# Reading w_ada's second third between the last six projections, and its last third behind the second scores

## What is computed

```
mod = silu(c) @ w_ada + b_ada            # w_ada: 1024 x 6144, 24 MB
sh_m, sc_m, gt_m, sh_f, sc_f, gt_f = split(mod, 6)
h    = rms_norm(x, g_pre_mix) * (1 + sc_m) + sh_m
proj = h @ w_in                          # q, k, v of branch a (8 heads) and of branch b (8 heads), forget gates
mix  = concat(fox_attention(a), moba_attention(b))
x    = x + gt_m * rms_norm(mix @ w_out, g_post_mix)
h    = rms_norm(x, g_pre_ffn) * (1 + sc_f) + sh_f
y    = mixture_of_experts(h)             # 32 experts, 4 of them per token, 12 MB of weights each
x    = x + gt_f * rms_norm(y, g_post_ffn)
```

## Time and profile before

| | |
|---|---|
| median of three runs | 2179.22 us (2178.69 to 2185.49) |
| span of the profiled execution | 2178.5 us (its device time is not listed apart; the span is 0.7 us under the median) |
| PE busy | 2000.2 us, 92% |
| DVE busy | 798.3 us, 37% |
| ACT busy | 704.7 us, 32% |
| DMA | 609.45 MB, mean 280 GB/s |
| mean granted TensorE clock | 0.963 |

### The profile page before, as it was taken

One profiled execution on the slowest core, in us unless ns is written; L12 is line 12 of the kernel. 1 busy time (PEld: TensorE's weight loads), 2 busy tenths in 40 slices (PEclk: granted clock), 3 DMA queues, 4 the chain that ended last, 5 costly groups with the idle time before them and its releaser, 6 DMA issues.

```text
span 2178.5 us, 30306 instructions
## 1 busy us (share of the span) xinstructions
PE 2000.2 (92%) x11645; PEld 1302.6 (60%) x11646; DVE 798.3 (37%) x1335; ACT 704.7 (32%) x1092; POOL 261.4 (12%) x246
## 2 busy tenths in 40 slices
PE   4997899999999999999999789997999799997998
PEld 2874433333333333333333388986998689987996
DVE  2544211111111111112111266416775474246763
ACT  1543112122222211111211246514554455315543
POOL 3400100000000010001000002000332020001340
PEclk7998699999999999999999989998999899998999
DMA  9956799998996999899999755434555454353553
GB/s 357 319 211 256 279 417 417 417 418 323 415 418 282 418 417 417 325 418 417 417 417 418 313 177 174 155 116 155 174 180 188 123 182 143 122 193 119 191 177 114
DMA packets 203055, 609.45 MB, mean 280 GB/s; under 512 B 10522, under 2 KB 115118, under 8 KB 166384
## 3 DMA queue, kind: packets, MB, share of 16 engines
q1 hardware_dynamic: 197600, 585.40, 70.3%
q0 software_dynamic: 5040, 21.89, 2.8%
q10 hardware_dynamic: 328, 0.95, 0.1%
HBM read 607.13 MB, written 9.26 MB: 283 GB/s over the span
## 4 chain that ended last, share of the span: by engine, by line
PE 70%; DMA 11%; DVE 5%; issue 5%; SPq 5%; ACT 3%; DVEq 0%; ACTq 0%
PE bank L744 32%; PE bank L1002 15%; PE bank L1031 9%; DMA ring<-in_w_gate_up 7%; PE bank L1095 3%; PE bank L962 2%; SPq L625 2%; SPq L628 2%; DMA ring<-in_w_in 2%; PE bank L975 1%; PE bank L995 1%; ACT probs L1587 1%; DMA ring<-in_w_ada 1%; DVE split L1424 1%; DVE probs L1152 1%
## 5 line engine op out<-in xcount | busy, mean ns | idle before, releaser
L1002 PE MATMUL bank<-ring,qkv 128*64 128x512 f32 x2240 | 496.6, 597 | 13.3 <-DMA ring<-in_w_gate_up 13.3
L744 PE MATMUL bank<-hT_hi,split 128*128 128x256 f32 x2432 | 442.7, 285 | 5.1 <-DVE hT_lo L1432 4.0
L744 PEld LDWEIGHTS bank<-hT_hi,split 128*128 128x128 f32 x2432 | 382.5, 194 | 7.9 <-issue 6.7
L1424 DVE TENSOR_TENSOR split<-ring,split 128x2048 fp32r<-128x2048 f32 x120 | 283.8, 2367 | 265.4 <-ACT split L1745 265.2
L1745 ACT ACTIVATE split<-ring 128x2048 fp32r<-128x2048 f32 x120 | 229.6, 1913 | 416.4 <-PE bank L744 327.8
L1002 PEld LDWEIGHTS bank<-ring,qkv 128*64 128x64 f32 x2240 | 155.3, 137 | 337.6 <-issue 294.8
L744 PE MATMUL bank<-hT_lo,split 128*128 128x256 f32 x1216 | 345.8, 284 | 0.0
L1031 PE MATMUL bank<-ring,qkv 128*64 128x512 f32 x1120 | 255.8, 598 | 25.7 <-ACT qkv L1706 23.5
L744 PEld LDWEIGHTS bank<-hT_lo,split 128*128 128x128 f32 x1216 | 235.2, 193 | 0.0
L1402 DVE SCALAR_TENSOR_TENSOR out_halves<-bank,probs,out_halves 64x512 fp32r<-64x512 f32 x70 | 52.5, 750 | 395.2 <-ACT out_halves L1728 394.7
L1392 DVE TENSOR_SCALAR qkv<-bank 128x512 f32<-128x512 f32 x35 | 24.2, 692 | 422.9 <-PE bank L1002 422.9
(11 more groups left out here) (284 smaller groups left out, 2278.7 us busy)
## 6 DMA issues: line engine op xcount, KB each, us to landing
ring<-in_w_gate_up SPq DMA_DIRECT2D x256, 1024.0 KB, 17.0
ring<-in_w_down SPq DMA_DIRECT2D x150, 1024.0 KB, 15.7
ring<-in_w_in SPq DMA_DIRECT2D x58, 1024.0 KB, 5.6
ring<-in_w_up SPq DMA_DIRECT2D x44, 1024.0 KB, 5.1
ring<-in_w_ada SPq DMA_DIRECT2D x24, 1024.0 KB, 8.3
ring<-in_w_out SPq DMA_DIRECT2D x12, 1024.0 KB, 6.4
ring<-in_w_branch SPq DMA_DIRECT2D x12, 1024.0 KB, 5.0
neighbours<-rpb_copies POOLq DMA_DIRECT2D x32, 128.0 KB, 8.4
```

Source lines behind the costliest of these rows:

```text
L744: last = pe.matmul(out, a[a_half], b[b_half], start=start and i == 0, stop=stop and i == 2)
L1002: last = pe.matmul(hidden[q][CAP * j:CAP * j + CAP, :], xgT[:, k % 4, k // 4, :], unit_at(k)[:, c:c + 512], start=False, stop=(k == KC - 1))
L1424: dve.tensor_tensor(low, unit_at(u % RING_L), high.bitcast(F32), ALU.subtract).then_inc(low_done, 1)
```

## The change

The order of the 40 units becomes: 8 of `ada0`; w_in's first six; then `qb0`, two of `ada1`, `qb1`, two of `ada1`, `kb0`, two, `kb1`, one, `vb0`, one, `vb1`; 8 of `ada2`; 4 of w_out. TensorE uses them in that order. The rows of `ada1` follow the scores of branch b, with all of `ada2` behind them and ahead of the values of b; the rows of `ada2` come between the second and the third unit of the product with w_out. VectorE copies the sums of `ada1` before `out_low("a")`, makes its rows between `keep_scores("b")` and `normalise`, and all four rows of `ada2` before `post_norm`. The sums of `ada1` move from `htok` to a part of `qkv`. The first expert's units wait slot by slot, and are issued in the order of slots 4, 5, 0, 1, 2, 3, then 8 to 11, then 6 and 7.

```diff
+FIRST_PART = 6
+BESIDE = dict(zip(IN1[FIRST_PART:], ((0, 2), (2, 4), (4, 6), (6, 7), (7, KC), (KC, KC))))
+
+def first_order():
+    order = [("ada0", k) for k in range(KC)] + [("in", u) for u in range(FIRST_PART)]
+    for u in range(FIRST_PART, len(IN1)):
+        order += [("in", u)] + [("ada1", k) for k in range(*BESIDE[IN1[u]])]
+    return order + [("ada2", k) for k in range(KC)] + [("out", u) for u in range(OUT_UNITS)]
+
+ORDER_1 = first_order()
+SPLIT_1 = [u for u, (kind, _) in enumerate(ORDER_1) if kind in ("in", "out")]
...
-        modrows = [probs_t[:, 2048:2560], htok_t[:, 0:512], qkv[:, 0:512]]
+        modrows = [probs_t[:, 2048:2560], qkv[:, 512:1024], qkv[:, 0:512]]
...  SP
+            sources = [parts[kind][i] for kind, i in ORDER_1]
...
             def first_wait(u):
-                if u == 0:
+                if u < RING:
+                    sp.wait_ge(unit_done, 1 + max(n for n in range(first.units) if n % RING == u))
+                if u == KC:
                     sp.wait_ge(unit_done, first.units)
                 if u == RING:
                     sp.wait_ge(h_ready, 4)
                     sp.wait_ge(*emptied("mod11"))
-            load_expert(0, first_wait)
+            ring_order = [n % RING for n in range(first.units - RING, first.units)]
+            load_expert(0, first_wait, [*ring_order, *range(KC, MOE_UNITS), *range(RING, KC)])
...  PE
             scores("a", proj1["qa"], lambda h, o: proj1["ka"][o:o + DH, h // 2, :], fox_bias)
-            project_set(IN1[6:])
+            for n in IN1[FIRST_PART:]:
+                project_set([n])
+                if BESIDE[n][0] < BESIDE[n][1]:
+                    ada_units(1, range(*BESIDE[n]))
             values("a", lambda h, c: proj1["va"][:, c, h * DH:h * DH + DH])
...
             scores("b", proj1["qb"], lambda h, o: proj1["kb"][o:o + DH, h // 2, :])
-            ada(1)
+            ada_rows(1)
+            ada_units(2, range(KC))
             values("b", lambda h, c: proj1["vb"][:, c, h * DH:h * DH + DH])
-            ada_units(2, range(KC // 2))
 
             def mixed_in(u):
+                if u == OUT_UNITS // 2:
+                    ada_rows(2)
                 read(*[f"{'ab'[u // 2]}out{2 * (u % 2) + i}" for i in range(2)])
 
             split_rows_product("mix", lambda f: (mix_hi[:, f, :], mix_lo[:, f, :]), KC, mixed_in)
-            ada_units(2, range(KC // 2, KC))
-            ada_rows(2)
...  DVE
             first_low(8, 9, 10, 11)
+            ada_sums(1)
...
             keep_scores("b", lambda tt, h: tables[:, tt, h, :])
+            ada_rows(1, 2 * [gate(gate_m, gpost_m)] + 2 * [shift(shift_f)])
             normalise()
-            ada(1, 2 * [gate(gate_m, gpost_m)] + 2 * [shift(shift_f)])
+            ada_sums(2)
             first_low(len(IN1), len(IN1) + 1)
             out_low("b")
             first_low(len(IN1) + 2, len(IN1) + 3)
+            ada_rows(2, 2 * [gain(gain_f, gpre_f)] + 2 * [gate(gate_f, gpost_f)])
+            await_own("mod5")
             post_norm([f"mix{j}" for j in range(4)], gate_m, x_mid)
-            ada(2, 2 * [gain(gain_f, gpre_f)])
+            await_own("mod7")
             await_own("mod9")
             await_x_mid()
             row_scale()
             modulated(gain_f, shift_f)
-            ada_rows(2, 2, 2 * [gate(gate_f, gpost_f)])
```

More of the change, by code:

```diff
@@ L203, in project, with project_beside, after_scores @@
             p.unit(n)
-    ada(0)
+    def project_beside():
+        p.bank("ada1")
+        for n in IN1[FIRST_PART:]:
+            project([n])
+            for k in range(*BESIDE[n]):
+                p.unit("ada1")
+    def after_scores():
+        ada_rows(1)
+        ada_units(2, KC)
+    ada_units(0, KC)
+    ada_rows(0)
     for l in range(LAYERS):
@@ L212, in plan_first @@
     p.tile("forget")
[L213 to L216, removed]
+    project(IN1[2:FIRST_PART])
+    p.attention("a", project_beside)
+    p.attention("b", after_scores)
     for j in range(4):
@@ L598, in _ @@
             w_out_v = w_out[0].rearrange("(k p) n -> p k n", p=P)
[L599 to L604, removed]
+            parts = {f"ada{r}": [w_ada[0, P * k:P * k + P, r * UNIT:(r + 1) * UNIT] for k in range(KC)] for r in range(3)}
+            parts["in"] = [w_in_v[:, :, 256 * u:256 * u + 256] for u in range(len(IN1))]
+            parts["out"] = [w_out_v[:, 2 * u:2 * u + 2, :] for u in range(OUT_UNITS)]
+            sources = [parts[kind][i] for kind, i in ORDER_1]
+            assert len(sources) == first.units
             for u, source in enumerate(sources):
@@ L614, in _, with load_expert @@
                 sp.dma_start(shape, source).then_inc(landed[s], 16)
-            def load_expert(e, wait):
+            def load_expert(e, wait, order=range(MOE_UNITS)):
                 wgu = w_gate_up[0, bass.ds(e, 1)].rearrange("e (k p) n -> (e p) k n", p=P)
                 wdn = w_down[0, bass.ds(e, 1)].rearrange("e (k p) n -> (e p) k n", p=P)
-                for u in range(MOE_UNITS):
+                for u in order:
                     wait(u)
-                    if u == 0:
+                    if u == order[0]:
                         sp.dma_start(brows, b_gate_up[0, bass.ds(e, 1)].rearrange("e (r n) -> (e r) n", r=4))\
@@ L879, in _ @@
             tile(last)
-            project_set(IN1[2:6])
-            read(*IN1[0:6])
+            project_set(IN1[2:FIRST_PART])
+            read(*IN1[0:FIRST_PART])
             pe.wait_ge(fox_ready, 1)
@@ L1197, in _, with ada_sums, ada_rows @@
             dve.wait_ge(gpre_in, 16)
-            def ada(r, takes):
+            def ada_sums(r):
                 await_full(f"ada{r}")
                 leave(dve.tensor_copy(modrows[r], bank(f"ada{r}")[:, :]), f"ada{r}")
-                ada_rows(r, 0, takes)
-            def ada_rows(r, first_row, takes):
-                for j, what in enumerate(takes, first_row):
+            def ada_rows(r, takes):
+                for j, what in enumerate(takes):
                     n, half = f"mod{4 * r + j}", slice(512 * (j % 2), 512 * (j % 2) + 512)
@@ L1227, in _ @@
             row_scale()
-            ada(0, 2 * [shift(shift_m)] + 2 * [gain(gain_m, gpre_m)])
+            ada_sums(0)
+            ada_rows(0, 2 * [shift(shift_m)] + 2 * [gain(gain_m, gpre_m)])
             await_own("mod1")
```

21 lines of the change are left out of this document (7 added, 14 removed).

## The result

The change made the kernel a little slower: 2186.65 us, the median of 20 runs (2178.38 to 2194.84), where the kernel before has 2179.6 (20 runs, 2177.28 to 2185.49). The ratio is 1.0027, interval 1.0019 to 1.0035. I had forecast 2176.1 and a range of 2171 to 2185; the time lies outside it.

What follows compares the result with a forecast made beforehand. TensorE's own work was taken as the bound nearly everywhere, so reordering wins only where it waits. +8.4 us to the values of b, -9.0 before the product, -0.6 in it, -1.95 behind: -3.1, 2176.1 us; range 2171 to 2185.

Steps and rivals of the forecast that it cites:

- step 1: `ada1` between the last projections: +8.27 us of work, +0.5 of waits, nothing for `qb1` (other end 3.6).
- step 2: Second scores to values of b: 16.44 us instead of 16.83, a gain of about 0.4.
- the sum: All stages up to h added: -3.1 us, from 2179.2 to 2176.1, with router and experts unchanged except their start.
- the three signs that I had named for being wrong: First scores after 97, product after 183, or h to first expert product not 33.9 us within 1.
- `qb1` is late: Rival at the first scores: they start 3.6 us later and all behind moves, 2179.7 us; chance 0.17.
- Starved: Rival in the last projections: POOL's packets also delay `kb0`, some 5 us; 2184.7, at worst 2189.9; chance 0.11.
- Steps 3 and 4: Product with w_out starts at 180.0, ends 203.1 against 204.28; behind it `row_scale` follows the root, -1.95, h at 215.8.
- Step 5: The experts' first units are asked for from 169 us instead of 208; gain nothing.
- a rival on the good side only: Router stage at a higher clock than 0.55: a quarter of 11.8 us, 3 us, goes; 2173.1; chance 0.12.

Runs made afterwards that it cites:

- x12: The kernel after, unchanged, measured and profiled a second time: 2186.21 us, ratio 1.0021 to the kernel before.
- x5: Kernel after, with POOL's 32 bias-table transfers waiting until ScalarE has made its sixteenth high half: 2183.89 us, ratio 1.0010 to the kernel before.
- x3: Kernel after, with `ada1`'s row matmuls behind the units of `ada2` and VectorE's rows behind `normalise`: 2184.58 us, ratio 1.0021 to the kernel before.
- x9: Kernel after, with `ada1` behind only `kb1`, `vb0`, `vb1`, its rows between `ada2`'s second and third unit, 13 constant products before the router: 2176.51 us, ratio 0.9977.
- x8: Kernel after, with `ada1`'s rows later, POOL's 32 copies delayed and 13 constant products after w_out's product: 2181.04 us, ratio 0.9999 to the kernel before.
- x10: Kernel after, with `ada1` behind only `kb1`, `vb0`, `vb1` and its rows between `ada2`'s second and third unit, no added products: 2178.44 us, ratio 0.9990.
- x4: Kernel after, with 13 added 128x512 products of constants behind the product with w_out: 2180.88 us, ratio 1.0007 to the kernel before.
- x7: Kernel after, with the first expert's twelve units issued as in the kernel before: 2189.68 us, ratio 1.0039 to the kernel before.
- x2: Kernel before's projections and `ada1`, only all of `ada2` moved ahead of w_out, expert's units waiting slot by slot: 2195.22 us, ratio 1.0062 to the kernel before.
- x11: Kernel before, with six added 128x512 products of constants ahead of its transposes of h: 2179.19 us, ratio 0.9990 to the kernel before.
- x1: `ada1` moved as in the kernel after, but `ada2` in two halves around w_out's product as in the kernel before: 2186.31 us, ratio 1.0028 to it.
- x6: Kernel after, with no w_ada unit between `qb0` and `qb1`, the eight spread over the other gaps: 2185.21 us, ratio 1.0015 to the kernel before.

## Why the prediction was wrong

The direction was wrong: -3.1 us forecast, about +6 to +7 measured (5.9 by the ratio, 7.05 between the medians, 5.6 between the spans). Three steps failed: step 1 put `qb1`'s lateness at nothing, step 2 gave the stage to the values of b 16.44 us at an unbroken clock, and the sum left the router's stage out as untouched. Of the three signs that I had named for being wrong two came: the product started at 187.04, after 183, and the router's stage took 36.0, not 33.9 within 1. The third, first scores after 97, did not come in this execution (96.44) and did in the next one (100.99, `x12`).

**Step 1, "I take nothing for it" (`qb1`).** Wrong in most executions. Eight profiles have `qb1` issued behind two w_ada units between 80 and 84 us. It landed 8.3 us later in the first profile of the kernel after and 11.6 in `x5`; in the other six it took 13.0 to 17.9, which is what the row of before had said (16.0). ScalarE's high half waited for it in these six, 0.7 to 5.6 us beyond the 3.4 that it waits anyway. I had argued the 16.0 away: a faster unit ahead would let `qb1` through before POOL's packets come. It did so once (the first profile of the kernel after, where this step cost nothing). The queues of `x12` from 90 to 91 us show how it fails; packets, MB, share of the engines:

```profile
q0 software_dynamic: 95, 0.36, 96.1%
q1 hardware_dynamic: 32, 0.03, 9.5%
```

POOL's packets fill the engines and the SP queue moves 0.03 MB in that microsecond, less even than the 0.10 of the earlier trace rows. So "equal packets" was not the lower limit of SP's part either. The rival "`qb1` is late" (2179.7) was true as a mechanism, but its price was short: in all six executions the clock fell to 1.2 GHz as well, and the first scores took 8.9 to 10.5 us instead of 7.2. That the longer wait brought the fall isn't shown, since it came without a longer wait too (last section).

**Step 1, the sum.** Forecast +8.77 between the two scores, measured +11.22. The bias and the eight units took 8.52 (0.99, three pairs of 1.85, two single ones of 0.99) instead of 8.27. The five projections that follow w_ada work take 5.95 to 5.99 each, where before, behind another projection, each took 5.76; `qb0`, behind the scores in both kernels, takes 5.94. That is +1.0 for the six. The first pair of matmuls after a switch takes 0.50 where the next ones take 0.40; the rest of the 0.2 I didn't trace. The waits are 1.66 instead of 0.5 (1.01 and 0.65): `kb0` landed after 7.2 us and `kb1`, issued at 118.49, after 6.9, where I had taken 5.3 from a place without rival queues. The row of the same moment had 6.7 and I had used it as the far end. In the seven other profiles with this order of units these waits were 0.4 to 1.3, so here the forecast was short by less than the first profile says. The DMA issues of the kernel after, from 81, 110 and 118 us (`qb1`, `kb0`, `kb1`; last number: us to landing):

```profile
ring<-in_w_in SPq DMA_DIRECT2D x1, 1024.0 KB, 8.3
...
ring<-in_w_in SPq DMA_DIRECT2D x1, 1024.0 KB, 7.2
...
ring<-in_w_in SPq DMA_DIRECT2D x1, 1024.0 KB, 6.9
```

"Starved" (2184.7, decided from 5.9 us of landing) came nearest in its number, by luck: the landing was past its point, but `kb0` cost 1.0 and not 5.

**Step 2, 16.44 us.** The count of work and transfers was right (16.0 in `x3`, 16.8 in `x9`), the place of the rows was not harmless. In the kernel after the row matmuls took 2.00 us instead of 1.14, while VectorE was still reading the banks of the scores (the weight load behind the rows waited 0.76 us for VectorE's L1158, which reads them). The clock fell to 1.2 GHz right behind them, from 163.4 to 170.2 us (mean 0.83 for the stage), the first units of `ada2` ran at half speed, so their slots came free late, and the last unit with them: from its first unit to its last 12.04 us where I had 9.56. It fell again in the values of b (5.38 for 32 matmuls that took 3.71). Four kernels with the rows behind at least two units of `ada2` (`x3`, `x8`, `x9`, `x10`) show no fall there. The six profiles with the rows ahead of the units (both of after, `x4` to `x7`) all do: the fall begins between 163 and 171 us, and the stage took 18.3 to 20.1 us where the four took 16.0 to 16.9. So the place of the rows decides for this order, six of six against none of four; how TensorE's clock responds to it is not shown. It can fall here without them: in `x2`, with the kernel before's order up to this point, it fell at 161 us, ahead of the rows, and the values of b took 10.3 us; in the kernel before and `x11` it did not. The Trainium skill (TensorE: Matmul & The Clock Gate, "A second HAM failure mode") has a kernel whose TensorE pauses shortly for PSUM between groups, with a clock that swings; the rows here, 2.00 us where `x3` took 1.14, agree with it.

**Steps 3 and 4, right.** The product began 1.34 behind the values, behind ScalarE's copies and the two halves, at full clock, in 23.36 us with the rows inside; forecast 1.8 and 23.1. From its end to h 12.90, forecast 12.7, with `row_scale` directly behind ScalarE's root. Without the rows the product took 22.2 at full clock, 0.4 more than my 21.8. Both steps stood 7 us later than forecast (187.0 and 223.3 instead of 180.0 and 215.8), by what came before them.

**Step 5, "gain nothing".** Not contradicted (`x7`).

**The router.** I had put its stretch beyond the change, as a rival on the good side only: a clock of more than 0.55. It went the other way: 36.0 us at 0.50. In the kernel before the clock was low as well when the transposes began, but it rose for 3.4 us (columns of the earlier trace rows):

```profile
219.00:221.80 2.80, 2.78 (x13) 2.80 (x14) 1.76 (x3) 1.20 (x2) 2.52 (x3) 0.50 1.01 427
221.80:225.20 3.40, 2.51 (x23) 2.30 (x22) 0.00 (x0) 2.38 (x3) 1.35 (x2) 1.00 1.04 352
225.20:252.80 27.60, 20.84 (x68) 11.39 (x67) 8.35 (x41) 3.38 (x8) 0.00 (x0) 0.50 0.59 238
```

In the kernel after it did not rise in the whole stage. There the work that step 4 took away as costless (`ada2`'s second half, run beside ScalarE and VectorE) no longer stands behind the product, and TensorE idles for 12.9 us. That this is where the 2.1 us come from is not shown: with the half in its place the stage took 33.8 (before) and 29.9 us (`x1`), and without it anything from 29.9 to 36.0. What the profiles do show is a shorter stage with work in the wait. In the eight profiles with that idle wait and nothing in it the stretch took 36.0 (five), 33.8 (two) and 29.9 (one); with products in the place 28.6 to 31.1 (four of four). In times the products are worth 4.4 us at the kernel after (1.0027 to 1.0007; their intervals overlap a little), 2.8 at `x10`, where the intervals overlap, and 2.2 at the kernel before, whose interval ends at 1.0000. The Trainium skill (TensorE: Matmul & The Clock Gate, "HAM oscillation — how this bites in real kernels") describes waits that make the next work start at the slow clock; `x4` and `x9` agree.

**What stays open.** The causes above were named from profiles; in the times only `x8`, `x9` and `x10`, each with more than one edit, are clear of the kernel after, so what each cause is worth alone is open. (a) What gives `x9` its 0.0022 over `x8`. In the profiles 2.4 us of the difference lie in the router's clock, 1.9 in the values of b (7.3 against 9.2, with VectorE's copy in time) and 1.1 in the projections; their shares of the times weren't separated. (b) The first scores, below. (c) Why 36.0, 33.8 or 29.9 with the same idle wait, and so what taking away `ada2`'s second half costs.

## What to carry to other kernels

Ahead of a move "into another unit's shadow", look whether the receiving stage has slack in its transfers at that very time, with every queue that is active there, and take the row of that time for the price, not the one from a quiet place. When work is removed from beside a wait, ask what clock the next stage will run at, and price it at both levels. Try thin work (row matmuls that wait for banks) between thick work, not ahead of it: here the clock fell in six of six profiles with it ahead and in none of four with it between or behind. And measure a filler against the old kernel with the same filler, or its gain is booked to the change.

## What I had not expected

- **The first scores.** In `x5`, `x6`, `x9` and `x10` ScalarE waits for nothing new (3.36 us, as before), TensorE's idle wait ahead of the first scores is 2.68 us as in the kernel before, and yet the clock is at 1.2 GHz from 95 to 102 us in `x9` and the scores take 8.9 to 10.5 us instead of 7.2. In the kernel before, `x2`, `x11` and the first profile of the kernel after, with the same 2.68 us, it stays at 2.4 GHz. The order of w_in's first six is the same in all of them; I found nothing in these profiles that tells them apart. It is worth up to 3 us, about half of the whole change. The Trainium skill (TensorE: Matmul & The Clock Gate, "Part 1: The HAM clock gate") says that the number of slow matmuls of one kernel varies from run to run; no run here can show whether that is it.
- **A gap can be cheap or dear.** A gap of 1.3 to 1.6 us ahead of the product cost no clock in any of ten profiles; the thin stretch of row matmuls, without an idle row of its own, was followed by a stage 4.0 us longer than `x3`'s (20.0 against 16.0).
- **Spread of the runs.** The kernel after spreads over 16.5 us, the kernel before over 8.2. `qb1`'s landing (8.3 to 17.9 us with one order of issue) is a part of it.
